# A two-layer hybrid transformer block with a Hyena layer on one core: sums of squares as two split products, and a new order of the modulation dots

## The reference

```
def rms_norm(x, gain=None):
    y = xf * lax.rsqrt(jnp.mean(xf * xf, axis=-1, keepdims=True) + RMS_EPS)
    ...
    mod = (cond @ w_ada[l] + b_ada[l])[:, None, :]
    h = rms_norm(x) * (1.0 + scale_a) + shift_a
    ...
    qh = (rms_norm(m_q, q_a_norm) @ w_q_up).reshape(B, S, MLA_HEADS, MLA_NOPE + MLA_ROPE)
    q_nope = rms_norm(q_nope, q_norm_nope)
    q_pe = apply_rope(rms_norm(q_pe, q_norm_rope), cos, sin)
    kv = (rms_norm(m_kv, kv_a_norm) @ w_kv_up).reshape(B, S, MLA_HEADS, MLA_NOPE + MLA_V)
    k_nope = rms_norm(k_nope, k_norm_nope)
    k_pe = apply_rope(rms_norm(m_kpe, k_norm_rope), cos, sin)
    mla_out = mla_attention(q_nope, q_pe, k_nope, k_pe, mv)      # 4 heads, causal, blocks of 128 queries
```

## Time and profile before

| | us |
|---|---|
| median of 3 runs (lowest, highest) | 4057.41 (4056.99, 4059.7) |
| the profiled execution | 4059.24 |
| its span, first to last instruction | 4057.1 |
| PE busy | 4008.6 |
| DVE busy | 2201.3 |
| ACT busy | 1476.9 |
| mean granted clock of PE | 0.996 of full |

### The profile page before, as it was taken

The page is one execution under the profiler, slowest core; times in us unless marked ns, Lnnn a source line. Parts: engine busy times, 40 slices in busy tenths (PEclk is TensorE's granted clock), DMA queues, the critical chain, the costliest instruction groups (busy, mean ns, idle before and its releaser), DMA issues.

```text
span 4057.1 us, 47421 instructions
## 1 busy us (share of the span) xinstructions
PE 4008.6 (99%) x18800; PEld 3079.5 (76%) x18800; DVE 2201.3 (54%) x3447; ACT 1476.9 (36%) x2424; POOL 106.4 (3%) x171
## 2 busy tenths in 40 slices
PE   9999999999999999999999999999999999999998
PEld 6777657888888877656888888777777777887786
DVE  7777576434434656566634334543546363646664
ACT  4433464212213333555412121333434343224533
POOL 2000000000000000000000000000000000000000
PEclk9999999999999999999999999999999999999999
DMA  7534101323332221201223221231111111116542
GB/s 253 202 104 135 50 1 42 96 94 101 94 104 75 87 79 47 72 10 37 63 83 94 75 71 47 73 109 47 37 47 47 40 46 63 43 58 222 187 161 77
DMA packets 99621, 342.13 MB, mean 84 GB/s; under 512 B 11016, under 2 KB 12072, under 8 KB 98250
## 3 DMA queue, kind: packets, MB, share of 16 engines
q1 hardware_dynamic: 78522, 258.87, 19.3%
q0 software_dynamic: 20880, 80.23, 6.2%
HBM read 304.45 MB, written 34.60 MB: 84 GB/s over the span
## 4 chain that ended last, share of the span: by engine, by line
PE 88%; DVE 7%; ACT 3%; issue 2%; DMA 0%; ACTq 0%; DVEq 0%; POOL 0%; POOLq 0%
PE PS L1305 35%; PE PS L1287 20%; PE PS L2393 4%; PE PS L2252 3%; PE PS L3289 2%; PE PS L3353 2%; PE PS L2162 1%; PE PS L1270 1%; PE PS L1690 1%; PE PS L1970 1%; PE PS L2683 1%; PE PS L1005 1%; PE PS L2130 1%; PE PS L2710 1%; PE PS L2696 1%
## 5 line engine op out<-in xcount | busy, mean ns | idle before, releaser
L640 ACT ACTIVATE WH<-raw 128x1024 fp32r<-128x1024 f32 x314 | 330.5, 1053 | 675.4 <-PE PS L1305 443.8
L1287 PE MATMUL PS<-hi,WH 128*128 128x512 f32 x1248 | 524.6, 420 | 0.4 <-DVE WL L651 0.2
L1305 PE MATMUL PS<-lo,WH 128*128 128x512 f32 x1312 | 515.0, 393 | 0.0
L1305 PE MATMUL PS<-hi,WL 128*128 128x512 f32 x1312 | 514.7, 392 | 0.0
L1305 PE MATMUL PS<-hi,WH 128*128 128x512 f32 x1312 | 513.0, 391 | 1.3 <-DVE WL L651 0.7
L1287 PE MATMUL PS<-hi,WL 128*128 128x512 f32 x1248 | 491.6, 394 | 0.0
L1287 PE MATMUL PS<-lo,WH 128*128 128x512 f32 x1248 | 488.5, 391 | 0.0
L651 DVE TENSOR_TENSOR WL<-raw,WH 128x1024 fp32r<-128x1024 f32 x274 | 334.9, 1222 | 127.3 <-ACT WH L640 127.2
L1305 PE MATMUL PS<-al,WH 128*128 128x512 f32 x768 | 301.8, 393 | 0.0
L1305 PE MATMUL PS<-ah,WH 128*128 128x512 f32 x768 | 300.7, 392 | 0.0
L1305 PE MATMUL PS<-ah,WL 128*128 128x512 f32 x768 | 300.3, 391 | 0.0
(11 more groups left out here) (478 smaller groups left out, 6939.1 us busy)
## 6 DMA issues: line engine op xcount, KB each, us to landing
adab<-in_w_ada POOLq DMA_DIRECT2D x120, 512.0 KB, 4.6
raw<-in_win SPq DMA_DIRECT2D x104, 512.0 KB, 3.6
raw<-in_down SPq DMA_DIRECT2D x80, 512.0 KB, 3.6
raw<-in_up SPq DMA_DIRECT2D x64, 512.0 KB, 3.6
raw<-in_dft SPq DMA_DIRECT2D x24, 512.0 KB, 4.1
sp_x<-X SPq DMA_DIRECT2D x24, 512.0 KB, 6.3
X<-sp_x SPq DMA_DIRECT2D x24, 512.0 KB, 5.0
raw<-in_wout SPq DMA_DIRECT2D x24, 512.0 KB, 3.6
```

The lines of the kernel that those rows point to most:

```text
L640: act.activation(PLACES[PLACE[j]][0], raw[:, j % 2, :], ACT.Copy).then_inc(*W_HI.next(j))
L1287: mm = pe.matmul(bank[b + hf], w[:, k, :], r[:, k, HALF[hf]], start=k == 0 and w is wh and r is hi, stop=k == 7 and w is wl)
L1305: mm = pe.matmul(bank[b + hf], w[:, k, :], r[:, k, HALF[hf]], start=k == 0 and w is wh and r is hi, stop=k == 7 and w is wl)
```

## The change

Three things change.

1. The sums of squares of the norm units of heads 1 to 3 (planned behind the start of head 0's attention) are split. ACT squares twice, once in f32 (into the lane's first scratch place) and once rounded to fp32r (into `SPLIT[lane][1]`); DVE subtracts the one from the other into `SPLIT[lane][0]`, in fp32r; PE multiplies remainder and rounded square with fp32r ones in two products into the same bank. PE's part is planned at 2.9 behind the unit's start instead of 1, ACT's logarithm at 3.6 instead of 2, DVE's Newton step at 6.0 (6.8 for the late unit of a head) instead of 4.5 (5.4), and the rotary norm's last step at 5.4 instead of 4. Lengths of the units and the times of their projections stay. The places are fp32r names of memory that was there before (`adab_r`, `pb_r`, `pT_r`).
2. The constants are loaded as before and then rewritten in place as fp32r by one ACT instruction in the opening; all later uses read that name (`const_r`), which in the f32 products holds the same values.
3. In the opening the planned times of the dots change, the last tile of x is loaded later, and the two bias products stand ahead of three spare products instead of behind. One dot of the linear attention is planned earlier.

```
-    opening = [23, 25.6, 28, 38.0, 38.6, 43, 50.8, 51.2, 64, 69, 76.8, 80.5, 89.1, 89.6, 99.5, 102.0]
+    opening = [23, 25.6, 28, 38.0, 38.6, 50.8, 64, 68, 72, 76.8, 79.2, 89.1, 89.6, 93.5, 99.5, 102.0]
...
-    free = [-1.0, 6.0] + [27.3 + 6.5 * i for i in range(7)] + [72 + 3.6 * i for i in range(6)] + [94.0, 97.0]
-    free += [114.3 + 6.4 * i for i in range(7)] + [156 + 3 * i for i in range(6)] + [173.5, 177.0]
+    free = [-1.0, 6.0] + [27.3 + 6.5 * i for i in range(7)] + [72 + 3.6 * i for i in range(6)] + [94.0, 97.0, 100.4]
+    free += [120.7 + 6.4 * i for i in range(6)] + [156 + 3 * i for i in range(6)] + [173.5, 177.0]
...
-            yield 64.0
+            yield 88.0
             sp.wait_ge(*WPM["low", 1, 1])
             sp.dma_start(X[:, 7, :], D["xT"][7 * P:8 * P, :]).then_inc(*X_IN.next(7, by=16))
...
-            spare_pe(pe, 5, 3, early)
             pe.wait_ge(*CONST[0])
             pe.wait_ge(*FBIAS_IN[0])
             for o in range(2):
-                pe.matmul(filter_bank(0, o), ident[0:1, :], m.fso[0:1, 0, o, :], start=True, stop=False)
+                pe.matmul(filter_bank(0, o), m.const[0:1, 0, :], m.fso[0:1, 0, o, :], start=True, stop=False)
+            spare_pe(pe, 5, 3, early)
...
+                u.split = kind in ("norm", "newton") and u.at > pair_at(l, 0, 0)
...
+        SPLIT = [(m.adab_r[:, 0, HALF[x]], m.adab_r[:, 1, HALF[x]]) for x in range(2)] + [(m.pb_r[:, 0:HS], m.pb_r[:, HS:S])]
+        SPLIT.append(tuple(m.pT_r[:, 4 * x:4 * x + 4, :].rearrange("p a b -> p (a b)") for x in range(2)))
+
+        def ones_act(act):
+            yield 50.0
+            act.wait_ge(*CONST[0])
+            act.activation(m.const_r[:, :, :], m.const[:, :, :], ACT.Copy).then_inc(*ML_ACT.next("ones"))
...
-                yield u.at + (1 if u.kind in ("norm", "newton") else 0)
+                yield u.at + (0 if u.kind not in ("norm", "newton") else 2.9 if u.split else 1)
...
+                    if u.split:
+                        pe.wait_ge(*ML_DVE["rest", l, lane, u.i])
+                        mat = m.const_r[0:u.rows, 2 if u.mat is m.onesbd else 1, 0:u.rows]
+                        for x, a in enumerate(SPLIT[lane]):
+                            mm = pe.matmul(PS[0:u.rows, b, :], mat, a[0:u.rows, :], start=x == 0, stop=x == 1)
+                        mm.then_inc(*ML_PE.next(l, lane, u.i))
+                        continue
...
+                    if u.split:
+                        sq = act.activation(SPLIT[lane][1][0:u.rows, :], u.src[0][0:u.rows, HALF[u.hf]], ACT.Square, bias=0.0)
                     sq.then_inc(*ML_ACT.next("square", l, lane, u.i))
-                    yield u.at + 2
+                    yield u.at + (3.6 if u.split else 2)
...
-                    yield u.at + (4 if u.kind == "norm" else 5.4 if u.late else 4.5)
+                    if u.split:
+                        yield u.at + 0.9
+                        dve.wait_ge(*ML_ACT["square", l, lane, u.i])
+                        high, low = SPLIT[lane][1][0:u.rows, :], SPLIT[lane][0][0:u.rows, :]
+                        dve.tensor_tensor(low, a1, high.bitcast(F), ALU.subtract).then_inc(
+                            *ML_DVE.next("rest", l, lane, u.i))
+                    yield u.at + ((5.4 if u.split else 4) if u.kind == "norm" else (6.8 if u.late else 6.0) if u.split else 5.4 if u.late else 4.5)
```

More of the change, by code:

```diff
@@ L340, in __init__ @@
         self.WL = sb(top, "WL", [P, 2, S], R)
+        with ExitStack() as c:
+            self.adab_r = sb(c, "adab_r", [P, 2, S], R)
+            sb(c, "gap3", [P, NVEC])
+            self.const_r = sb(c, "const_r", [P, 4, P], R)
         self.adab = sb(top, "adab", [P, 2, S])
@@ L343, in __init__ @@
         self.const = sb(top, "const", [P, 4, P])
-        self.ident, self.ones, self.onesbd, self.rotm = (self.const[:, i, :] for i in range(4))
+        self.ident, self.ones, self.onesbd, self.rotm = (self.const_r[:, i, :].bitcast(F) for i in range(4))
         self.negm = sb(top, "negm", [P, P])
@@ L404, in __init__ @@
                 self.el = sb(c, "el", [P, 8])
+            with ExitStack() as c:
+                sb(c, "gap5", [P, 9, S])
+                sb(c, "gap6", [P, HS])
+                self.pb_r = sb(c, "pb_r", [P, S + HS], R)
+                self.pT_r = sb(c, "pT_r", [P, 12, P], R)
             with ExitStack() as c:
@@ L554, in build @@
         FN_ACT, FN_DVE, OUT = signal("final_act"), signal("final_dve"), signal("out_stored")
-        SPARE = m.const[:, :, :].rearrange("p a b -> p (a b)")
+        SPARE = m.const_r[:, :, :].bitcast(F).rearrange("p a b -> p (a b)")
         def spare_pe(pe, b, n, x=SPARE):
@@ L756, in setup_sp @@
             sp.dma_start(m.w4[:, :, :, :].rearrange("p a b c -> p (a b c)"), D["fw4"]).then_inc(*W4_IN.next(0, by=16))
-            for dst, name in ((ident, "ident"), (ones, "ones"), (m.onesbd, "onesbd"), (m.rotm, "rotm"), (m.negm, "negm")):
-                sp.dma_start(dst[:, :], D[name]).then_inc(*CONST.next(0, by=16))
+            for i, name in enumerate(("ident", "ones", "onesbd", "rotm", "negm")):
+                sp.dma_start(m.const[:, i, :] if i < 4 else m.negm[:, :], D[name]).then_inc(*CONST.next(0, by=16))
             sp.dma_start(m.fso[0:1, 0, :, :], D["fbias"]).then_inc(*FBIAS_IN.next(0, by=16))
@@ L1845, in build @@
             late: bool = False
+            split: bool = False
         LONG = {"norm": 5.0, "newton": 7.5, "project": 2.5, "rotate": 3.5, "copy": 1.0, "exchange": 0.9, "values": 3.0}
@@ L1942, in build, with ones_pe @@
         SCRATCH.append(tuple(m.pT[:, 4 * x:4 * x + 4, :].rearrange("p a b -> p (a b)") for x in range(2)))
+        SPLIT = [(m.adab_r[:, 0, HALF[x]], m.adab_r[:, 1, HALF[x]]) for x in range(2)] + [(m.pb_r[:, 0:HS], m.pb_r[:, HS:S])]
[4 more added lines that the diff above has]
+            act.activation(m.const_r[:, :, :], m.const[:, :, :], ACT.Copy).then_inc(*ML_ACT.next("ones"))
+        def ones_pe(pe):
+            yield FIRST_SUMS - 0.1
+            pe.wait_ge(*ML_ACT["ones"])
         def mla_sp(sp, l):
@@ L3524, in pe_program @@
         def pe_program(pe):
-            in_order(setup_pe(pe), filters_pe(pe), filter_spectra_pe(pe), *norms(first_norm_pe, half_norm_pe, pe), spare_norm_pe(pe), *per_layer(win_first_pe, pe), *per_layer(win_pe, pe),
+            in_order(setup_pe(pe), filters_pe(pe), filter_spectra_pe(pe), ones_pe(pe), *norms(first_norm_pe, half_norm_pe, pe), spare_norm_pe(pe), *per_layer(win_first_pe, pe), *per_layer(win_pe, pe),
                      *per_layer(win_values_pe, pe), *per_layer(gla_decays_pe, pe), *per_layer(gla_levels_pe, pe),
@@ L3542, in act_program @@
             in_order(weights_act(act), setup_act(act), setup_weights_act(act), filters_act(act), filter_spectra_act(act), first_squares_act(act),
-                     *norms(first_norm_act, half_norm_act, act), *per_layer(win_act, act), rope_act(act), *per_layer(mixer_table, act),
+                     ones_act(act), *norms(first_norm_act, half_norm_act, act), *per_layer(win_act, act), rope_act(act), *per_layer(mixer_table, act),
                      *per_layer(gla_decays_act, act), *per_layer(gla_outputs_act, act), *per_layer(gla_squares_act, act),
```

## The result

| | before | changed |
|---|---|---|
| median of 4 runs (lowest, highest), us | 4057.20 (4054.09, 4059.70) | 4088.68 (4086.13, 4091.49) |
| the profiled execution, us | 4059.24 | 4090.5 |
| its span, us | 4057.1 | 4088.4 |
| mean granted clock of PE | 0.996 | 0.992 |

The ratio is 1.0075, 95% interval 1.0063 to 1.0087: the changed kernel is 31.5 us slower. The forecast was 4079, 22 slower; its range reached to 4096. A second series of the same kernel gave 1.0074 (1.0062 to 1.0087).

The account below looks back on a forecast made before the run. PE was taken as the bound, busy 4008.6 of 4057.1 us. 4059.2 + 23 (attention) - 2.4 (opening) - 1.1 (dot) + 2 (clock) = 4080.7, less 1.8 for the median: 4079; range 4061 to 4096.

Parts of the forecast that it names:

- The chain in the attention: Latent attention, heads 1 to 3: PE waits for later ACT and DVE steps; net +11.4 us a layer, +23 in all.
- The walk: Following the attention's new order with the profile's durations: 23.3 us of PE idle a layer.
- The walk of the old order: The same hand-following of the attention's order before the change: 6.4 us of PE idle a layer.
- The products saved: Split sums in the attention: two fp32r products take 0.46 instead of 0.85 us; 28 sums save 10.9 us of PE.
- The clock: Half clock of PE after ten idles of 2.35 or 2.6 in both layers' attention: 0 to 18, taken as +2 us.
- every long idle trips the clock: Rival, attention: half clock follows all ten long idles, +18 instead of +2 us, giving 4095; chance 0.13.
- The opening: Opening: moved dots end DVE's work earlier, shortening PE's 3.28 us wait; -2.4 us taken, PE winning 0 to 5.1.
- The moved dot: Linear attention: one dot leaves DVE ahead of steps PE waits 1.67 us for; about -1.1 us, 0 to -2.9.
- PE busy 11 lower: Sign to look for in the changed profile: PE's busy time lower by about 11 us.
- my mark of under 1 us: Sign to look for in the opening: PE's wait for ft under 1 us.
- One sum of a rival: Rival, split sums: fp32r products cost as f32, 28 x 0.85 us on top, at most 4100; chance under 0.02.

Follow-up runs that it names:

- e6: The changed kernel with spare f32 products filling the idles ahead of second-half mkv projections and the keys' second sums; 4077.2 us, ratio 1.0044.
- e3: The changed kernel with its new places kept, but one square, no subtraction and one f32 product per sum; 4066.7 us, ratio 1.0019.
- e2: The changed kernel with the old opening, old dots and old order of bias products, only the split sums new; 4089.3 us, ratio 1.0074.
- e1: The changed kernel with its sums of squares unsplit as before; new opening, moved dots and rewritten constants stay; 4053.4 us, ratio 0.9985.
- e5: The changed kernel with only the rounded square, no subtraction and one fp32r product per sum, at the old places; 4039.7 us, ratio 0.9952.
- e7: The changed kernel with its split sums at the best of 192 placings walked through on paper; 4085.7 us, ratio 1.0067.
- e4: The changed kernel with the steps of its split sums put back to the old places; 4099.5 us, ratio 1.0097.
- e10: The changed kernel with two spare f32 products ahead of the second-half mkv projections only; 4080.0 us, ratio 1.0058.
- e8: The changed kernel without DVE's subtraction; the second fp32r product takes the rounded square again, doubling the sums; 4080.1 us, ratio 1.0049.

## Why the prediction was right, and where it was off

The prediction said slower, by 22 us; it was 31. Its sum, term by term, in the profiled executions:

- **The chain in the attention: right.** The walk gave 11.4 us a layer at full clock; e6, which has the change's order and full clock, shows 11.0 and 10.8. The single idles read a little shorter than forecast: 0.48 for 0.8 ahead of mq,wq; 2.31 for 2.6 ahead of mkv,VT; 1.01, 2.04 and 2.71 for 1.4 and twice 2.35 ahead of the keys' second sums; 1.03 for 1.3 and 1.45 for 1.8 in head 1; 0.4 for 0.8 ahead of the products of values. Part of that is the reading: the idle in brackets counts from the end of a record, and records overlap. Counted as the walk counts, from 499.28 plus 1.3 for the scores to 503.05, the idle ahead of mkv,VT is 2.5. The walk of the old order was too high in the same way, 6.4 where the brackets of the trace give 3.7, so most of that error left the difference.
- **The products saved: right.** "Two of them are 0.46", and a sum saves 0.39: e3 against the changed kernel shows 1.03 less 0.64 and 2.68 less 2.28. So the spacing inside a long run of fp32r products also held for a pair between f32 products, and 28 sums give the 10.9.
- **The clock: the step that failed.** "The new order has ten idles of 2.35 or 2.6 ... I take 2". Seven of the ten were followed by half clock, 18.8 us in the windows, 15.1 on the path by e6. The reason given, that f32 work of full height lies around them, does not hold. The rival "every long idle trips the clock" had the bound 18 and was given 0.13; that the windows lost 18.8 is luck in part, as it was four stretches of 3.4 and three of 1.7, not ten of 1.8. With 15 in place of 2 the forecast would have been 4092. The terms as measured, 21.8 + 15.1 - 1.4 - 2.7 - 1.6 = 31.2, are the 31.3 between the two profiled executions.
- **The opening: right in kind, its size not settled by one execution.** Here it is -1.4 for -2.4. But the ten experiments with the new opening give -0.5 to -4.5 against the same profile of before, the smallest gains where they have most half clock in it, and the middle of all eleven is -3.2; e2, with the old opening, gives -0.3. The wait of 3.28 is gone, PE is busy for 40.0 of the 40 us from 60 to 100 (36.7 before) and at full clock. The last product of the filters' transform starts 3.1 us earlier (136.96 for 140.10). Then 1.7 are given back, as the working had it, at the first products behind the norm, which wait for DVE; half clock of 1.7 us follows there, at 141.5. The changed kernel's timeline on PE has the row

```profile
140.94 0.47 PE L1314 MATMUL PS<-hi,WH 128*128 128x512 f32 x1 [2.10 <-DVE lo L1174]
```

  where before three such waits came to 1.24. The longest wait for ft that is left, 1.3 at 33.18, misses my mark of under 1 us.
- **The moved dot: right, -1.1; the rest of the -2.7 is luck.** The wait fell from 1.67 to 0.53, which is the 1.1; the other 1.6 is the half clock behind it. e2 shows that this part was not the dot's to give: it kept the wait and lost no clock. And e1, e3, e5, e6 and e7, with the dot moved, have half clock elsewhere in the linear attention and win 1.1 or 1.2 there.
- **PE busy 11 lower: hidden by the slow clock.** It rose by 1.5, since slow products are busy longer. e3 and e6 have full clock in both attentions and the same half clock ahead of them: 4003.6 with f32 sums, and 4013.1 with split ones and 22 spare products. Less 22 x 0.86 for the spare ones that leaves 3994, 9 to 10 lower (an estimate).
- **One sum of a rival was wrong.** If fp32r products cost as f32 ones do, two take 1.70 where the forecast has 0.46. That is 28 x 1.24 = 35 on top of it, not 28 x 0.85, and 4114 instead of "at most 4100", outside the range. Nothing of it happened.

## What to carry to other kernels

When an engine's list already ends on time, follow the new order of all the engines with durations from the trace; here that gave the cost of a new wait chain within 0.6 us a layer, while counting the saved products had the wrong sign. Then give the idles that the new order adds on TensorE a term and a range for the half clock that may follow them, 1.7 or 3.4 us a stretch in these traces, before believing the sum: their length did not tell which were followed, and some of 1.0 to 1.5 us were. And where a cheaper product needs extra steps to make its operands, first ask whether the remainder is needed at all: the version without it was the fast one. And read what a short product costs from the products around it in two kernels of one order, not from the start of its own record.

## What the runs showed of the chip that was not expected

- A pair of fp32r products of 512 columns between f32 products costs 0.46 us, twice the 0.23 of a long run of them, but the record of the first can begin 0.03 to 0.09 us behind the start of the product ahead of it, so that from its own start to the next product's it reads 0.56 or 0.87.
- Spare products can make a kernel faster: e6 has 22 more of them and is 12.6 us (0.31%) ahead of the changed kernel by the ratios.
- How long an idle is does not tell whether half clock follows. Six idles of 1.75 in e3 were followed by none, ten of 2.04 to 2.71 in the changed kernel by seven stretches, ten of 2.70 to 3.09 in e4 by five, and of four of 2.05 in e10 three; in e8 idles of 1.03 and 1.54 were followed by it. The same idle of 1.7 in the linear attention was followed by one in the profile before and by none in e2, and five kernels have a stretch there with no idle over 0.5 us in the 25 us ahead.
